# Routing lists built in two parts, sums over tiles as products with ones, and modulation pieces taken in pairs

## The reference

```
proj = rms_norm(h, g_mix) @ w_in                  # 512 x 3072
...
mod = silu(cond) @ w_mod + b_mod                  # two layers, two conditions: 2 x 3072 each
...
g_prob = softmax(xf @ w_rg)                       # 4 groups, the best one is taken
e_w, e_i = top_k(softmax(e_logits), 2)            # the best 2 of its 8 experts
weights = g_gate * (e_w / sum(e_w))
experts = g_idx * 8 + e_i
...                                               # rows sorted by expert, blocks of 128 rows
hdn = silu(xb @ w1[e]) * (xb @ w3[e])             # 1024 -> 512
ys = hdn @ w2[e]                                  # 512 -> 1024
out[row] += ys * weight
...
h + rms_norm(p @ w_ple, g_ple) * sigmoid(rms_norm(h, g_plg) @ w_plg)
```

## Time and profile before

| | |
|---|---|
| median of 3 runs | 1835.11 us (1831.62 to 1835.55) |
| profiled execution, its own time | 1840.27 us |
| its span in the profile | 1838.5 us |
| granted TensorE clock, mean | 0.991 |
| TensorE matmul busy | 1757.7 us (96%) |
| weight loads, VectorE, ScalarE, GpSimd busy | 966.1, 750.5, 553.3, 154.0 us |
| moved by DMA | 324.85 MB |

### The profile page before, as it was taken

One profiled execution on the slowest core, in us unless ns is written; L12 is line 12 of the kernel. 1 busy time (PEld: TensorE's weight loads), 2 busy tenths in 40 slices (PEclk: granted clock), 3 DMA queues, 4 the chain that ended last, 5 costly groups with the idle time before them and its releaser, 6 DMA issues. The chain is left out here.

```text
span 1838.5 us, 24632 instructions
## 1 busy us (share of the span) xinstructions
PE 1757.7 (96%) x9830; PEld 966.1 (53%) x9830; DVE 750.5 (41%) x1600; ACT 553.3 (30%) x1119; POOL 154.0 (8%) x194
## 2 busy tenths in 40 slices
PE   8999988998989899999989999999999999999998
PEld 3333465454544444555564444577745644466663
DVE  2243477241521221333223325377624337466642
ACT  2111378222101111333223212355412233344420
POOL 0320001001111101111000014000000002100000
PEclk9999989999999999999999999999999999999999
DMA  8565778438999999999981222000021012000001
GB/s 277 210 216 183 115 150 82 152 133 329 420 416 416 417 416 418 418 418 417 400 326 65 92 92 92 1 1 2 23 84 35 24 40 83 32 2 1 2 24 46
DMA packets 92194, 324.85 MB, mean 177 GB/s; under 512 B 12312, under 2 KB 28824, under 8 KB 65072
## 3 DMA queue, kind: packets, MB, share of 16 engines
q1 hardware_dynamic: 78224, 302.55, 45.3%
q10 hardware_dynamic: 8656, 12.32, 2.0%
q0 software_dynamic: 5200, 8.41, 1.2%
HBM read 317.58 MB, written 14.30 MB: 181 GB/s over the span
## 5 line engine op out<-in xcount | busy, mean ns | idle before, releaser
L1099 PE MATMUL mix_ps<-arena 128*64 128x256 f32 x2048 | 238.4, 385 | 8.8 <-DMA arena<-in_w 4.8
L2186 PE MATMUL tail_ps<-arena 128*128 128x512 f32 x488 | 213.4, 592 | 0.9 <-DMA arena<-in_w_plg 0.9
L1099 PEld LDWEIGHTS mix_ps<-arena 128*64 128x64 f32 x2048 | 145.2, 138 | 95.5 <-issue 23.3
L987 PE MATMUL mix_ps<-arena,side 128*128 128x512 f32 x384 | 175.9, 611 | 0.6 <-DMA arena<-in_w_in 0.6
L498 DVE TENSOR_SCALAR_CACHE_REDUCE arena<-tail_ps 128x768 f32<-128x768 f32 x128 | 117.5, 955 | 105.9 <-PE tail_ps L358 67.0
L2186 PEld LDWEIGHTS tail_ps<-arena 128*128 128x128 f32 x488 | 91.8, 190 | 111.4 <-issue 110.9
L1111 PE MATMUL mix_ps<-arena 128*64 128x512 f32 x512 | 118.6, 605 | 22.3 <-DMA arena<-in_w 22.3
L987 PEld LDWEIGHTS mix_ps<-arena,side 128*128 128x128 f32 x384 | 72.3, 194 | 102.5 <-issue 84.2
L2186 PE MATMUL tail_ps<-arena,side 128*128 128x512 f32 (+2 forms) x328 | 123.6, 535 | 0.0
L585 ACT ACTIVATE arena<-arena,tail_small 128x768 f32<-128x768 f32 x128 | 118.2, 927 | 4.5 <-DVE arena L498 4.5
L377 PE MATMUL tail_ps<-first,arena 128*128 128x128 f32 x768 | 97.9, 277 | 0.5 <-ACT arena L585 0.5
(11 more groups left out here) (406 smaller groups left out, 2385.9 us busy)
## 6 DMA issues: line engine op xcount, KB each, us to landing
arena<-in_w SPq DMA_DIRECT2D x96, 2048.0 KB, 21.1
arena<-in_l_w_mod SPq DMA_DIRECT2D x16, 1024.0 KB, 5.1
arena<-in_l_w_in SPq DMA_DIRECT2D x16, 1024.0 KB, 7.3
arena<-in_w_in SPq DMA_DIRECT2D x12, 1024.0 KB, 9.2
arena<-in_l_w_mod SPq DMA_DIRECT2D x16, 512.0 KB, 4.7
residual<-bias_blocks SPq DMA_DIRECT2D x32, 224.0 KB, 12.6
arena<-in_l_w_in ACTq DMA_DIRECT2D x12, 512.0 KB, 11.1
arena<-in_l_w_out SPq DMA_DIRECT2D x6, 1024.0 KB, 5.1
```

Of the source, the lines that this page charges most:

```text
L987: last = pe.matmul(ps[:, u % 4], oT[:, k, t * P:(t + 1) * P], weights.slot(W_IN[n, k // 4], 4, 512)[:, k % 4], start=(k == 0), stop=(k == ...
L1099: last = pe.matmul(out[h * CAP:(h + 1) * CAP, 0:H2], x, wb[:, k, h * H2:(h + 1) * H2], start=(k == 0), stop=(k == DK - 1))
L2186: last = pe.matmul(out, lhs(k), rhs(k), start=(k == 0), stop=(k == K - 1))
```

## The change

1. **Routing's list is made twice.** A first list multiplies `hot` with `told_read` (row to read, 32 columns, bank 2) and gives `index[:, 0]`; the second multiplies with the two other products (64 columns, bank 3). Weights, `count` and these two products move behind the rank. `told`, `sel` and `rank` are one instruction for both experts instead of two. The load of expert 0's `w2` waits for the second list, and `indexed` 2 is waited for one step earlier (L1118 instead of L1127). ACT's exponential of `gap` moves behind its second emptying.
2. **Sums over tiles as products of ones.** `A_sum` and its five instructions go. `A_all` has a fifth, empty tile; one product with `before` over 160 columns and four with `ones` over 128, 96, 64 and 32 columns (the same tile repeated) give ranks and counts in one place.
3. **`beside` goes by single units:** 3 before `chosen`, 1 after `ranked`, 2 between the lists, 2 after the second.
4. **Modulation in pairs.** Pieces u-1 and u run together after every second unit. Odd pieces have a place of their own, a sixth slot in `work` (columns 6144 to 8191, where the squares of x lie at first), so piece i waits for piece i-2, and piece 1 for the squares.
5. Two semaphores are merged (`silu`, `lam_exp` into `act_small`).

```diff
-SLOT, SLOTS = 2048, 5
+SLOT, SLOTS = 2048, 6
...
-    weights = Weights(ring, s["loaded"])
+    weights = Weights([view(ring, i * SLOT, SLOT) for i in range(SLOTS - 1)] + [view(work, 6144, SLOT)], s["loaded"])
...
-            W_MOD[i] = weights.add(0, (s["mod_mm"], i) if i else None, *of)
+            W_MOD[i] = weights.add(5 * (i % 2), (s["mod_mm"], i - 1) if i >= 2 else (s["x_squared"], XT) if i else None, *of)
...
-            sp.wait_ge(s["listed"], 1)
+            sp.wait_ge(s["listed"], 2)
             expert(0, "w2")
...
-                    modulate(u)
+                    if u % 2:
+                        modulate(u - 1)
+                        modulate(u)
...
-            for t in range(2):
-                beside(t)
+            for u in range(3):
+                beside(u)
             pe.wait_ge(s["chosen"], 1)
-            pe.matmul(ps[:, 4, 0:XT * N_EXPERTS], m["before"], A_all.rearrange("p t e -> p (t e)"), start=True, stop=False)
-            pe.matmul(ps[:, 4, 0:XT * N_EXPERTS], m["ones"], A_sum[:, 0:XT].rearrange("p t e -> p (t e)"), start=False, stop=True)
-            pe.matmul(ps[:, 4, 256:256 + N_EXPERTS], m["ones"], A_sum[:, XT], start=True, stop=True).then_inc(s["ranked"], 1)
-            beside(2)
+            blocks = (XT + 1) * N_EXPERTS
+            pe.matmul(ps[:, 4, 0:blocks], m["before"], A_all.rearrange("p t e -> p (t e)"), start=True, stop=False)
+            for t in range(XT):
+                last = pe.matmul(ps[:, 4, (t + 1) * N_EXPERTS:blocks], m["ones"], A_all[:, t].unsqueeze(1).to_broadcast([P, XT - t, N_EXPERTS]),
+                                 start=False, stop=(t == XT - 1))
+            last.then_inc(s["ranked"], 1)
+            beside(3)
...
-            list_slots(4, hot, told, 3 * N_EXPERTS, s["hot"], s["listed"])
-            beside(3)
+            list_slots(ps[:, 2, 0:N_EXPERTS], hot, lambda x, t: told_read[:, x, t], s["hot"], s["listed"])
+            beside(4)
+            beside(5)
+            pe.wait_ge(s["hot"], 3)
+            list_slots(ps[:, 3, 0:2 * N_EXPERTS], hot, lambda x, t: told[:, x, t].rearrange("p v e -> p (v e)"), s["hot"], s["listed"])
+            beside(6)
+            beside(7)
...
+            dve.memset(A_all[:, XT], 0.0)
...
-            chain(dve.tensor_tensor(A_all, flat(O[:, 0]), flat(O[:, 1]), ALU.add))
-            chain(dve.memset(A_sum[:, 0], 0.0))
-            for t in range(XT - 1):
-                chain(dve.tensor_tensor(A_sum[:, t + 1], A_sum[:, t], A_all[:, t], ALU.add))
-            dve.tensor_tensor(A_sum[:, XT], A_sum[:, XT - 1], A_all[:, XT - 1], ALU.add).then_inc(s["chosen"], 1)
+            dve.tensor_tensor(A_all[:, 0:XT], flat(O[:, 0]), flat(O[:, 1]), ALU.add).then_inc(s["chosen"], 1)
+            chain(dve.tensor_tensor(told_read, both, each(wide_row(m["read_row"], N_EXPERTS)), ALU.mult))
+            dve.wait_ge(s["ranked"], 1)
+            chain(dve.tensor_tensor(sel, both, each(ps[:, 4, 0:XT * N_EXPERTS].rearrange("p (t e) -> p t e", t=XT)), ALU.mult))
+            chain(dve.tensor_reduce(rank, sel, AX.X, ALU.add))
...
+            dve.wait_ge(s["listed"], 1)
+            chain(dve.tensor_tensor(slot_rows, ps[:, 2, 0:N_EXPERTS], m["spare_row"].to_broadcast([P, N_EXPERTS]), ALU.add))
+            dve.tensor_copy(index[:, 0], slot_rows).then_inc(s["indexed"], 1)
+            for k, told_of in enumerate((m["write_row"].rearrange("p (x t) -> p x t", x=2), vals)):
+                last = dve.tensor_tensor(told[:, :, :, k], both, told_of.unsqueeze(3).to_broadcast([P, 2, XT, N_EXPERTS]), ALU.mult)
+            last.then_inc(s["hot"], 1)
```

More of the change, by code:

```diff
@@ L627, with __init__ @@
 class Weights:
-    def __init__(self, ring, loaded):
-        self.ring, self.loaded = ring, loaded
+    def __init__(self, places, loaded):
+        self.places, self.loaded = places, loaded
         self.pieces, self.due, self.in_slot = [], [], [0] * SLOTS
@@ L644, in load @@
         for first, dims, src in pieces:
-            sp.dma_start(view(self.ring, slot * SLOT + first, *dims), src).then_inc(self.loaded[slot], 16)
+            sp.dma_start(view(self.places[slot], first, *dims), src).then_inc(self.loaded[slot], 16)
     def arrived(self, pe, i):
@@ L714, in first_layer @@
     gap = routing(XT)
-    A_all, A_sum = routing(XT, N_EXPERTS), routing(XT + 1, N_EXPERTS)
+    A_all = routing(XT + 1, N_EXPERTS)
     sel = routing(2, XT, N_EXPERTS)
-    hot, told = routing(2, XT, 2, CAP), routing(2, XT, 3, N_EXPERTS)
+    hot, told_read, told = routing(2, XT, 2, CAP), routing(2, XT, N_EXPERTS), routing(2, XT, 2, N_EXPERTS)
     slot_rows, slot_rows_2 = view(small, 632, N_EXPERTS), view(small, 664, N_EXPERTS)
@@ L1046, in _, with beside, list_slots @@
             pe.wait_ge(s["side_in"], 16)
[L1048 to L1056, removed]
-            for t in range(2):
-                beside(t)
-            pe.wait_ge(s["chosen"], 1)
-            pe.matmul(ps[:, 4, 0:XT * N_EXPERTS], m["before"], A_all.rearrange("p t e -> p (t e)"), start=True, stop=False)
-            pe.matmul(ps[:, 4, 0:XT * N_EXPERTS], m["ones"], A_sum[:, 0:XT].rearrange("p t e -> p (t e)"), start=False, stop=True)
-            pe.matmul(ps[:, 4, 256:256 + N_EXPERTS], m["ones"], A_sum[:, XT], start=True, stop=True).then_inc(s["ranked"], 1)
-            beside(2)
-            def list_slots(bank, lhs, rhs, n, done, listed):
+            def beside(u):
+                t, cc = u // 2, u % 2
+                if u >= 3:
+                    pe.wait_ge(s["side_ev"], u - 2)
+                for k in range(2):
+                    last = pe.matmul(ps[:, 5 + u % 3], side_in[:, k, t * P:(t + 1) * P], weights.slot(W_PLE, 2, D)[:, k, cc * 512:(cc + 1) * 512],
+                                     start=(k == 0), stop=(k == 1))
+                last.then_inc(s["side_mm"], 1)
+            for u in range(3):
+                beside(u)
+            pe.wait_ge(s["chosen"], 1)
+            blocks = (XT + 1) * N_EXPERTS
[5 more added lines that the diff above has]
+            beside(3)
+            def list_slots(out, lhs, rhs, done, listed):
                 for x in range(2):
@@ L1117, in hidden @@
                     pe.wait_ge(s["h_taken"], e)
+                else:
+                    pe.wait_ge(s["indexed"], 2)
                 turn_hidden().then_inc(s["hid_turned"], 1)
@@ L1601, in _ @@
             chain(dve.tensor_tensor(vals[:, 1], vals[:, 0], gap, ALU.mult))
[L1602 to L1606, removed]
-            for x in range(2):
-                chain(dve.tensor_tensor(sel[:, x], flat(O[:, x]), ps[:, 4, 0:XT * N_EXPERTS].rearrange("p (t e) -> p t e", t=XT), ALU.mult))
-                chain(dve.tensor_reduce(rank[:, x], sel[:, x], AX.X, ALU.add))
-            chain(dve.tensor_copy(count, ps[:, 4, 256:256 + N_EXPERTS]))
-            for x in range(2):
-                dve.tensor_tensor(hot[:, x].rearrange("p t a r -> p t (a r)"), m["count"].unsqueeze(1).to_broadcast([P, XT, 2 * CAP]),
-                                  rank[:, x].unsqueeze(2).to_broadcast([P, XT, 2 * CAP]), ALU.is_equal).then_inc(s["hot"], 1)
+            dve.wait_ge(s["listed"], 1)
[4 more added lines that the diff above has]
+            last.then_inc(s["hot"], 1)
             def rows_to_write(told_row, n, tmp, to):
```

42 lines of the change are left out of this document (24 added, 18 removed).

## The result

The changed kernel takes 1825.42 us (median of 13 runs, 1821.54 to 1832.39). The kernel before took 1835.55 in the runs beside it (13 runs, 1831.62 to 1840.9). The ratio is 0.9941 [0.9928, 0.9953], so 10.8 us faster (8.6 to 13.2); the medians are 10.1 apart. The forecast was 1821.7, range 1814 to 1829. The direction and the range held, and both mechanisms show in the traces; the size was 2.6 too large by the ratio, and the trace has a fall of the clock that the forecast did not have.

The account below looks back on a forecast made before the run. Bound by TensorE's step in the projection, VectorE's chain and a gather in routing, bytes in the experts; 8.1 us from modulation (3.6 + 4.5) plus 5.3 from routing gave 13.4 off 1835.11, so 1821.7 us, range 1814 to 1829.

Parts of the forecast that it names:

- Bounds: Input projection set by TensorE's step, routing by VectorE's chain then a gather, experts by bytes; earlier gains pass to the end.
- Pairs, 3.6: Input projection: 12 pairs of modulation pieces each pay the 0.30 us of changing over once, saving 3.6 us.
- The rule of the Trainium skill that was weighed against it: Weight loads overlap running matmuls only where row groups differ; pairing would then save about 2.4 us.
- The first four units, 4.5: Start of the input projection: removing the third piece's 2.8 us wait and 1.7 us of slow clock saves 4.5 us.
- Routing, 5.3: Indices out 3.15 us earlier and no TensorE wait for the gather: expert 0's `w1` product and weight stream 5.3 us earlier.
- The statement that gather and TensorE are ready together: Before the first expert: TensorE free at 416.7, about when the gathered rows land (416.6, taking 7.2 us).
- The forecast is wrong if the clock falls in new places: Sign against the forecast anywhere in the changed kernel; listed beside a pair waiting for DMA or a longer stream; no size given.
- The second pair: Rival in the first four units: pieces and constants share the DMAs, TensorE idles and slows; up to 4.5 us, chance 0.13.
- the near end: Loads of pieces 2, 3 and constants at 434 GB/s take 8 us, leaving 5 us to spare before the second pair.
- The rule of the Trainium skill named with it: DMAs of all issuing engines run on the same 16 engines and interleave, which would favour the second pair waiting.
- TensorE was in the way in routing: Rival: eight units and two lists in one queue hold up the first expert; costs 3 to 4 of 5.3 us, chance 0.13.
- Later pairs: Rival in the input projection: five pairs wait behind 2 MB chunks, 22.5 us lost against 13.4 saved, 1844 us; chance 0.04.

Follow-up runs that it names:

- the slot alone: Kernel before with the sixth slot and earlier piece loads, but still one piece after each unit and the old routing: 1834.99 us, ratio 0.9979.
- routing edits alone: Changed kernel with the old modulation (five slots, one piece after each unit): 1833.04 us, ratio 0.9982 to the kernel before.
- sums alone: Kernel before with only the sums over tiles made as products of ones, without the five VectorE instructions: 1836.49 us, ratio 1.001.
- units moved behind the list: Kernel before with its fifth and sixth side units run behind routing's list, in TensorE's wait for the first gather: 1838.94 us, ratio 1.0007.
- before + 2.3 us: Kernel before with 2.3 us of extra, overwritten products in the output projection's last unit, ahead of the router: 1841.35 us, ratio 1.0016.
- modulation alone: Kernel before with six slots, pieces in pairs and merged semaphores, routing as before: 1832.31 us, ratio 0.9963.

## Why the forecast was right, and where its size was off

**Bounds.** Right. The projection goes by TensorE's step, the experts by bytes: 416 GB/s in both, and from the `w1` product of expert 0 to the first product after the experts are 524.9 us before and 525.0 after. What is won ahead of the stream passes through. That the start of the stream is what counts holds only while nothing behind it is held up: with two units behind the first expert's products the same stretch took 528.4.

**Pairs, 3.6.** Right: 0.31 a pair in the steps, 3.6 between the slot alone and the pairs. The rule of the Trainium skill that was weighed against it ("TensorE: Matmul & The Clock Gate", Part 3, The mechanism) would have given 2.4; the trace disagrees, since 16 narrow passes take 1.90, which leaves nothing bare between the pieces.

**The first four units, 4.5.** This is the step that was mis-sized. The mechanism is shown (the sixth slot alone removes the wait), but 2.8 of wait and 1.7 of clock were read from one execution, and both vary. Five executions with the old modulation show them as follows; these are rows of TensorE's timeline with the routing edits alone, and with the sums alone:

```profile
37.28 1.04 PE L969 MATMUL mix_ps<-arena,mix_small 128*2 128x512 f32 x8 [0.85 <-DMA arena<-in_l_w_mod]
38.25 7.13 PE L987 MATMUL mix_ps<-arena,side 128*128 128x512 f32 x16
```

```profile
38.55 1.04 PE L969 MATMUL mix_ps<-arena,mix_small 128*2 128x512 f32 x8 [2.43 <-DMA arena<-in_l_w_mod]
39.52 7.13 PE L987 MATMUL mix_ps<-arena,side 128*128 128x512 f32 x16
```

| execution | wait | next unit | projection ends |
|---|---|---|---|
| before | 2.75 | 8.83 | 210.01 |
| units moved behind the list | 2.24 | 8.78 | 209.44 |
| sums alone | 2.43 | 7.13 | 208.25 |
| before + 2.3 us | 2.31 | 7.13 | 208.23 |
| routing alone | 0.85 | 7.13 | 207.30 |

The mean wait is 2.1 and the mean clock loss 0.7 (1.7 in two of five), together 2.8, not 4.5: the wait was short in one. The profiled execution of before was the worst in both, and the forecast took its price off a median that does not pay it. The ends come near: mean 208.65 with the old modulation, 201.70 with pairs, 6.95 between them where 8.1 was forecast, beside the 6.8 timed for modulation alone. Of the 0.5 that 6.95 has over 3.6 and 2.8, nearly all is there before the second piece: it starts 1.64 earlier with pairs on the mean, of which the piece no longer ahead of it explains 1.16. Why, no run shows.

**Routing, 5.3.** Right where the clock holds over the router: 5.5 there, and nothing in sum where it falls. Routing alone has its indices cast 5.65 behind `A_all` (forecast 5.3, though the steps of the forecast add up to 5.5; before 8.67) and its `w1` product 18.9 behind `A_all` (forecast 19.1, before 24.5). In the changed kernel the cast comes 7.1 behind, since the units ahead of the ranks ran at half clock. The statement that gather and TensorE are ready together was wrong: with the queue shorter the rows were in use after 3.6 us, with idle DMAs, so 7.2 was indeed only an upper bound and TensorE's queue set the turn.

**The clock over the router, not in the sum.** "The forecast is wrong if the clock falls in new places": it did. From the router's first product to the end of `A_all` are 13.7 us in the eight profiles with full clock and 17.7 to 18.2 in the six with 0.50, so about 4.2 up to there. The cost goes on behind it, in the units and lists: to expert 0's `w1` product four profiles with the new routing and the fall need 38.5, and routing alone, without it, 32.6, so 5.9 in all, more than routing wins. It stands in six of the eight profiles of kernels with pairs and in none of the six without. Among the timed executions it must be rarer, if the other terms are right: in three of four it would cost 4.4 of the 11.8 summed below and leave 7.4, under the interval. Two things agree with that. All six profiled executions with the fall are in the slower half of their kernel's runs. And their mean granted clock is 0.989 to 0.993, while 7 of the 19 timed executions of the changed kernel have 0.995 or more; these took 1821.3 to 1824.0, the other twelve 1823.9 to 1832.4.

**The sum again.** 3.6 + 2.8 for modulation, 0.1 less for the wait inside the first pair (0.69 in the changed kernel's profile, under 0.4 in the seven others), and 5.5 for routing: 11.8, against the measured 10.8 (8.6 to 13.2). The mis-sized term brings the sum into the interval. The 1.0 that remains would fit the low clock in about one of ten executions and the 0.5 given back behind the experts, but it is smaller than the interval, and this is argued, not shown. The range tests this sum weakly: 15 us wide, it holds every gain from 6 to 21.

**The rivals.** The second pair did not wait for a DMA, in any of eight profiles. (The 5 us that the forecast gave as the near end to spare is 7 by its own numbers, 15.3 less 8.) The rule of the Trainium skill named with it ("DMA: Bandwidth & Descriptors", Issuing engines are not separate DMA queues) found no case here: the one late piece, the first pair's second, was issued at 21.9 and there at 27.0. These 5.1 us are no more than such pieces take at the median (5.1 before, 6.1 in the changed kernel). TensorE was in the way in routing (13 of 100), in part: its queue, not the gather, sets the turn of expert 0, and the same two units behind the second expert bring 3 us more; but the 5.3 came all the same, as the queue ended as early as was forecast. Later pairs never waited.

**What stays open.** Why the half clock comes over the router, and whether kernels with pairs have it more often. A fixed place in the kernel's own time does not explain it; a place against the steps of the clock would, and no run tests that. Neither the sixth slot alone nor the routing edits alone show the fall in their one profile each, which says little. More executions of each kernel with a profile would be needed to say whether six of eight against none of six is more than a tendency.

## What to carry to other kernels

A stall and the low clock behind it, read in one execution, have a spread of their own: before such a term is taken off a median, look for the same place in other executions, above all when the profiled one lies above the median. Where two engines hand work to and fro, an edit that shortens one side pays only if the other's queue is cut to fit: the sums alone gave nothing in the trace, filling the idle time alone gave nothing that could be measured, and both together with a split list and a new order of the units gave 5.5 at full clock. And when an idle wait has been filled with work, ask whether the filler is now what is waited for; here two of eight units moved behind the second expert gave 3 us more, and moved only behind the first they showed no gain in the trace. Last, two profiles are compared stretch by stretch only after their clocks: a fall in one of them here hid the whole gain of routing.

## What the runs showed of the hardware

- TensorE's granted clock went to 0.50 and stayed there from some 383.5 to 397 us although the engine was busy before and throughout, in products of 36 columns first. The same products ran at 1.00 in the kernel with the routing edits alone. A timeline that shows no idle time is no proof of full clock; the windows have to be read as well.
- An indirect gather needed at most 3.6 us from issue to use where the load of `w2` came behind it; with the load of `w2` in flight ahead of it the rows were used after 7.2.
- The first narrow piece behind full-width products costs 0.86 of passes and 0.30 of changing over and back; the second behind it only its 0.86.
